# Latent and stick-breaking heads of one layer in one pipeline of head pairs

## The reference, cut to what matters

```python
def block(i):                       # stick-breaking, 128 queries
    z = einsum('bhqd,bhkd->bhqk', qb, k) * scale
    mask = k_idx[None, :] < q_idx[:, None]
    log_beta = log_sigmoid(z)
    log_1m_beta = where(mask, log_sigmoid(-z), 0.0)
    suffix = cumsum(log_1m_beta, reverse=True) - log_1m_beta
    a = where(mask, exp(log_beta + suffix), 0.0)
    return einsum('bhqk,bhkd->bhqd', a, v)

def even_mixer(...):
    mla = causal_softmax_attention(q, k, v, MLA_QK ** -0.5)
    sb = stick_breaking_attention(sq, sk, sv)
    return concatenate([merge_heads(mla), merge_heads(sb)], -1) @ w_o
```

## Time and profile before

| | |
|---|---|
| median of 3 runs | 2231.72 us |
| profiled execution | 2235.53 us |
| its span | 2233.8 us |
| PE, PEld busy | 93%, 75% |
| DVE, ACT, POOL busy | 40%, 25%, 49% |
| granted TensorE clock, mean | 0.941 |
| `att2` | from 997.5 us to 1046.2 us of the span |
| `stk` | from 1046.2 us to 1156.3 us |
| `x2` and `out2` begin | 1156.8 us and 1159.6 us |
| `fox` | from 1736.1 us to 1816.1 us |

### The profile page before, as it was taken

How to read it: one execution, slowest core, us unless ns; L and a number is a source line. 1 busy time by engine, 2 the same in 40 slices (tenths; PEclk the granted TensorE clock), 3 DMA queues, 4 the chain that set the end, 5 groups by cost and what they waited for, 6 DMA issues and landing times.

```text
span 2233.8 us, 30365 instructions
## 1 busy us (share of the span) xinstructions
PE 2066.8 (93%) x10488; PEld 1671.8 (75%) x10488; DVE 883.7 (40%) x1588; ACT 552.6 (25%) x1376; POOL 1084.4 (49%) x703
## 2 busy tenths in 40 slices
PE   5776999789999998979999999999899899999999
PEld 4666676678888887757668888888688568888887
DVE  4664567255434016456664212100462634121200
ACT  2111556232223003336542101000221522011100
POOL 5443003247666655400025766656465345666663
PEclk9886998889999999989569999999999999999999
DMA  4212001123233223210012333323232012333322
GB/s 137 64 61 66 0 0 38 40 64 104 94 97 119 86 81 89 64 38 1 1 38 76 104 94 98 99 85 103 54 100 85 30 39 72 108 94 95 102 91 88
DMA packets 125372, 161.96 MB, mean 73 GB/s; under 512 B 11670, under 2 KB 87398, under 8 KB 125286
## 3 DMA queue, kind: packets, MB, share of 16 engines
q1 hardware_dynamic: 121440, 159.97, 22.8%
q10 hardware_dynamic: 3846, 0.82, 0.2%
HBM read 158.66 MB, written 2.10 MB: 72 GB/s over the span
## 4 chain that ended last, share of the span: by engine, by line
PE 85%; DVE 8%; ACT 3%; issue 2%; POOL 1%; DMA 1%; ACTq 0%; SPq 0%; DVEq 0%; POOLq 0%
PE ps L653 22%; PE ps L654 22%; PE ps L655 22%; PE ps L1061 5%; PE ps L1082 4%; PE ps L1073 2%; PE ps L668 2%; PE ps L786 1%; PE ps L1066 1%; PE ps L1011 1%; DVE tok L1768 1%; PE ps L1089 1%; PE ps L1190 1%; DVE xt_lo L1778 1%; ACT dump L1309 1%
## 5 line engine op out<-in xcount | busy, mean ns | idle before, releaser
L435 POOL TENSOR_TENSOR w_lo<-raw,w_hi 128x1024 fp32r<-128x1024 f32 (+1 forms) x256 | 614.9, 2402 | 21.3
L433 POOL TENSOR_SCALAR w_hi<-raw 128x1024 fp32r<-128x1024 f32 (+1 forms) x256 | 276.0, 1078 | 546.6 <-PE ps L655 530.2
L653 PE MATMUL ps<-xt_hi,w_hi 128*128 128x512 f32 (+1 forms) x1160 | 434.2, 374 | 7.2 <-DVE xt_lo L1778 6.4
L654 PE MATMUL ps<-xt_lo,w_hi 128*128 128x512 f32 (+1 forms) x1160 | 433.4, 374 | 0.0
L655 PE MATMUL ps<-xt_hi,w_lo 128*128 128x512 f32 (+1 forms) x1160 | 433.2, 373 | 0.0
L653 PE MATMUL ps<-w_hi,xt_hi 128*128 128x512 f32 (+3 forms) x672 | 263.5, 392 | 28.8 <-ACT tok L1604 19.4
L654 PE MATMUL ps<-w_lo,xt_hi 128*128 128x512 f32 (+3 forms) x672 | 259.0, 385 | 0.0
L655 PE MATMUL ps<-w_hi,xt_lo 128*128 128x512 f32 (+3 forms) x672 | 258.9, 385 | 0.0
L653 PEld LDWEIGHTS ps<-xt_hi,w_hi 128*128 128x128 f32 x1160 | 220.5, 190 | 47.1 <-DVE xt_lo L1778 7.6
L655 PEld LDWEIGHTS ps<-xt_hi,w_lo 128*128 128x128 f32 x1160 | 220.3, 190 | 38.5
L654 PEld LDWEIGHTS ps<-xt_lo,w_hi 128*128 128x128 f32 x1160 | 220.4, 190 | 38.4
(11 more groups left out here) (310 smaller groups left out, 2771.4 us busy)
## 6 DMA issues: line engine op xcount, KB each, us to landing
raw<-in_w_up SPq DMA_DIRECT2D x88, 256.0 KB
raw<-in_l_w_gate SPq DMA_DIRECT2D x88, 256.0 KB
raw<-in_l_w_up SPq DMA_DIRECT2D x88, 256.0 KB
raw<-in_l_w_down SPq DMA_DIRECT2D x40, 512.0 KB
raw<-in_l_w_in SPq DMA_DIRECT2D x36, 512.0 KB
raw<-in_w_down SPq DMA_DIRECT2D x20, 512.0 KB
raw<-in_l_w_o SPq DMA_DIRECT2D x16, 512.0 KB
raw<-in_w_in SPq DMA_DIRECT2D x12, 512.0 KB
```

Of the source, the lines that this page charges most:

```text
L433: e.tensor_scalar(w_hi[:, s, 0:width], r, 1.0, 0.0, ALU.mult, ALU.add).then_inc(split, 1)
L435: e.tensor_tensor(w_lo[:, s, 0:width], r, w_hi[:, s, 0:width].bitcast(F32), ALU.subtract).then_inc(split, 1)
L653: e.matmul(o, s_hi, m_hi, start=start, stop=False)
L654: e.matmul(o, s_hi, m_lo, start=False, stop=False)
```

## The change

`att2`, `stk` and `x2` are gone. One pipeline `mix` of 8 pairs takes their place, in the form of `fox`: pairs 0 to 3 are the latent heads (`soft`), pairs 4 to 7 the stick-breaking ones. The class `Pairs` gives the rounds of both `fox` and `mix`; 32 steps (a pair's 4 blocks of 512, 384, 256 and 128 keys) run in 40 rounds, the weights of a soft step are turned 2 rounds after its scores, those of a stick step 3 rounds after. `fox` keeps its order on every engine.

- The latent heads' scores contract 96 rows, so the two heads of a pair can't lie above each other; they run one after the other. Their keys lie in `km_a` and `km_b`.
- A stick step: PE scores of two heads side by side (queries and keys 128 rows high, `qs` and `ksb`, now 4 tiles of 128 rows turned with half as many transposes), ACT Sigmoid of the negated scores, DVE a running product from the row's end into `runs` (`products`), POOL the difference of neighbours into the tile of weights (`sticks`), PE transposes, ACT nearly all copies of turned weights (`turner`), PE values. ACT and DVE split the output to high and low (`high`, `low`).
- ACT loads the sigmoid's table before step 16 and the exp and ln table at the end.
- In `act_pair_attend` the copies of turned weights stand ahead of the newest probabilities of the same round.
- POOL splits the four slabs of `out2`'s first group in rounds 3, 7, 11 and 15. SP's order stays, row for row.
- Staging of queries on POOL and the matmuls of no use (`fill` in `stk`) are gone; 8 of them remain at the start.

```diff
-        stage_queries(e, "att2", lambda hd: heads(qm, hd), MQK, 4, ...)
-        stage_queries(e, "stk", lambda hd: heads(qs, hd), HD, 4, [], ("att2", 32))
-        split_all(e, ph["out2"])
+        pool_pairs(e, mix, {3 + 4 * s: (ph["out2"].g0, s) for s in range(4)})
+        split_all(e, ph["out2"], 1)
...
+        def turn_round(self, g):
+            return g + (2 if self.is_soft(g) else 3)
+        def values_round(self, p):
+            return 4 * p + (9 if p < self.soft else 10)
+    fox = Pairs("fox", 8, 8, fox_rooms)
+    mix = Pairs("mix", 4, 8, mix_rooms)
...
+        def sticks(g):
+            for x in range(2):
+                u = 2 * (g - 4 * st.soft) + x + 1
+                e.wait_ge(*at(f"{name}_sc", u))
+                r = run_at(g, x)
+                n = (4 - g % 4) * P
+                e.tensor_tensor(prob_at(g, x), r[:, 1:n + 1], r[:, 0:n], ALU.subtract).then_inc(sem(f"{name}_w"), 1)
...
-        alternate([(64 * i, HD, qs[:, i, :]) for i in range(8)]),
+        alternate([(P * i, P, qs[:, i, :]) for i in range(4)]),
...
+    def turner(st, g, y):
+        if st.is_soft(g):
+            return "a" if y == 1 and g % 4 in (0, 3) else "d"
+        return "d" if y == 0 and g == 4 * st.soft + 3 else "a"
...
+    def mix_scores(e, p, i, b):
+        n = (i + 1) * P
+        if p < mix.soft:
+            for x in range(2):
+                hd = 2 * p + x
+                e.matmul(bank(b[x], n), qm[:, hd, i * P:(i + 1) * P], (km_a, km_b)[hd // 4][:, hd % 4, 0:n],
+                         start=True, stop=False)
+            for x in range(2):
+                m = e.matmul(bank(b[x], P, i * P), ident_b[:, :], causal[:, :], start=False, stop=True)
+            return m
+        for x, r in enumerate(HALVES):
+            e.matmul(bank(b[x], n), qs[r, p - mix.soft, i * P:(i + 1) * P], ksb[r, p - mix.soft, 0:n],
+                     start=True, stop=False)
+        return half_masks(e, b, i * P, strict, strict_x)
...
-        pe_attend(e, att["att2"])
-        pe_attend(e, att["stk"])
-        pe_out(e, "out2", "x2_lo", ...)
+        pe_pair_attend(e, mix, mix_scores, heads_of(v2), [at("in2_tpa", 12), at("in2_tpd", 15), at("in2_copy", 32)], [])
+        pe_out_direct(e, "out2", [at("mix_lo", 2), at("mix_lo", 4), at("mix_slo", 2), at("mix_slo", 4)], ...)
...
+                else:
+                    e.wait_ge(*at(f"{name}_s", g + 1))
+                    e.activation(prob_at(g, x), src, ACT.Sigmoid, scale=-1.0).then_inc(*od.done(*done))
...
+        for r in st.rounds:
+            if r == 4 * st.soft and r < st.steps:
+                e.preload_act_table(ACT.Sigmoid)
+            for g in st.turned_in(r):
+                turned(g)
+            for p in st.pair_in(r, st.inverse_round, range(st.soft)):
+                inverses(p)
+            if r < st.steps:
+                probs(r)
...
+        def products(g):
+            n, h = (4 - g % 4) * P, g - 4 * st.soft
+            for x in range(2):
+                e.wait_ge(*at(f"{name}_p", 2 * g + x + 1))
+                if h >= 4:
+                    e.wait_ge(*at(f"{name}_w", 2 * (h - 4) + x + 1))
+                e.tensor_tensor_scan(run_at(g, x)[:, 0:n][:, ::-1], prob_at(g, x)[:, ::-1],
+                                     one[:, 0:1].broadcast_to([P, n]), 1.0, ALU.mult, ALU.mult).then_inc(
+                    *od.done(*at(f"{name}_sc", 2 * h + x + 1)))
```

More of the change, by code:

```diff
@@ L493, in widened, with halves @@
             e.tensor_copy(inv_w[:, :, :], inv[:, :].unsqueeze(2).broadcast_to([P, 8, HD])).then_inc(sem(f"{name}_iw"), 1)
[L495 to L500, removed]
+        def halves(p):
             e.wait_ge(*at(f"{name}_x", p + 1))
@@ L506, in pool_pairs @@
                 sem(f"{name}_lo"), 1)
+        def sticks(g):
[6 more added lines that the diff above has]
+        for r in st.rounds:
+            for p in range(st.soft):
+                if r == 4 * p + 5:
+                    widened(p)
+            if r in slabs:
+                split_slab(e, *slabs[r], SLAB)
+            for p in range(st.soft):
+                if r == max(4 * p + 11, st.inverse_round(p) + 2):
+                    halves(p)
+            if st.is_soft(r - 1) or r - 1 >= st.steps:
+                continue
+            sticks(r - 1)
     def stage_queries(e, ph, q_src, rows, iters, ready, before=None):
@@ L592, in _ @@
         e.tensor_copy(pick[:, :, :], pick8[:, :].unsqueeze(2).broadcast_to([P, 8, P])).then_inc(picks, 1)
-        pool_pairs(e, "fox", 8, {s: (ph["out3"].g0, s) for s in range(4)})
+        pool_pairs(e, fox, {9 + 4 * s: (ph["out3"].g0, s) for s in range(4)})
         split_all(e, ph["out3"], 1)
@@ L1033, in pe_pair_attend, with half_masks @@
-            if g >= 9 and g % 4 == 1:
-                values((g - 9) // 4)
+                    e.wait_ge(*is_turned(st, st.steps - 1, y))
+                    e.wait_ge(*at(f"{name}_r{'ad'[y]}", st.pairs - 1))
+                turn_inverses(st.pairs - 1).then_inc(sem(f"{name}_ri"), 1)
+            for p in st.pair_in(r, st.values_round, range(st.pairs)):
+                values(p)
+    HALVES = (slice(0, HD), slice(HD, P))
+    def half_masks(e, b, last, mask, mask_x):
+        for x, r in enumerate(HALVES):
+            e.matmul(bank(b[x], P, last), ident_b[r, :], mask[r, :], start=False, stop=False)
+        for x, r in enumerate(HALVES):
+            m = e.matmul(bank(b[x], P, last), ident_x[r, :], mask_x[r, :], start=False, stop=True)
+        return m
@@ L1046, in fox_scores @@
-        for x, r in enumerate(halves):
-            m = e.matmul(bank(b[x], P, last), ident_x[r, :], causal_x[r, :], start=False, stop=True)
-        return m
+        return half_masks(e, b, i * P, causal, causal_x)
     def pe_attend(e, cfg):
@@ new lines, in high @@
+        def high(p):
+            e.wait_ge(*at(f"{name}_o", p + 1))
+            e.activation(xt_hi[:, p, :], bank(6), ACT.Copy).then_inc(*od.done(*at(f"{name}_shi", p + 1 - st.soft)))
+        for r in st.rounds:
+            if r == 4 * st.soft and r < st.steps:
+                e.preload_act_table(ACT.Sigmoid)
+            for g in st.turned_in(r):
+                turned(g)
+            for p in st.pair_in(r, st.inverse_round, range(st.soft)):
+                inverses(p)
+            if r < st.steps:
+                probs(r)
+            for p in range(st.soft, st.pairs):
+                if r == st.values_round(p) + 1:
+                    high(p)
@@ L1576, in _ @@
+        if st.soft < st.pairs:
+            e.preload_act_table_set(EXP_LN)
     @block.scalar
@@ new lines, in low @@
+        def low(p):
+            e.wait_ge(*at(f"{name}_shi", p + 1 - st.soft))
+            e.tensor_tensor(xt_lo[:, p, :], bank(6), xt_hi[:, p, :].bitcast(F32), ALU.subtract).then_inc(
+                *od.done(*at(f"{name}_slo", p + 1 - st.soft)))
+        for r in st.rounds:
+            if r == 4 * st.soft and r < st.steps:
+                e.wait_ge(*at(f"{name}_s", r + 1))
+                for g in range(r, r + 4):
+                    n = (4 - g % 4) * P
+                    e.memset(runs[:, :, RUN_AT[g % 4] + n:RUN_AT[g % 4] + n + 1], 1.0).then_inc(*od.own())
+            if r < st.steps:
+                (maxima if st.is_soft(r) else products)(r)
+            for p in range(st.soft):
+                if r == 4 * p + 4:
+                    inverses(p)
+            for g in st.turned_in(r):
+                turned(g)
+            for p in st.pair_in(r, st.inverse_round, range(st.soft)):
+                turned_inverse(p)
+            for p in range(st.soft):
+                if r == max(4 * p + 10, st.inverse_round(p) + 1):
+                    scaled(p)
+            for p in range(st.soft, st.pairs):
+                if r == st.values_round(p) + 1:
+                    low(p)
```

316 lines of the change are left out of this document (128 added, 188 removed).

## The result

| | before | after |
|---|---|---|
| median (lowest to highest) | 2231.8 us (2231.17 to 2232.52, 4 runs) | 2167.09 us (2165.19 to 2172.37, 4 runs) |
| profiled execution, its span | 2235.53, 2233.8 us | 2167.14, 2165.3 us |
| first scores of the new pipeline's place | 997.53 us | 994.01 us |
| first matmul of `out2` | 1159.57 us | 1095.50 us |
| last low part before `up2` | 1224.46 us | 1158.77 us |

The ratio is 0.9714, 95% interval 0.9697 to 0.9731: 64 us faster. The forecast was 2162, range 2148 to 2180. The stage that was 162.0 us long is 101.5 us long (forecast 97.5).

A forecast was written before the change was run, and what follows sets the result against it. Stick half before: a loop through four engines at PE's low clock; after: DVE and POOL excluding each other. Stage 162.0 to 97.5 us (-64.5), with -1.9 and -3.5 together -69.9: 2165.6 profiled, 2162 median, range 2148 to 2180.

The forecast's parts named there:

- the way out: End of the stage: a short transposition, two copies and one pair's values, 4.5 us in all.
- the way in: From step 16's scores to the first running product: about 2 us, the table's load standing beside the scores.
- the soft half: Latent heads, pairs 0 to 3: 10.2 us a pair, bounds 9.3 and 11.5; step 16's scores 36.0 us after the start.
- the stick half: Stick-breaking pairs 4 to 7: 13.0 us a pair, bounds 11.3 and 16; 52 us for four, plus 3 for POOL's leftovers.
- `in2`, -3.5 us: Input projection: half as many transposes of stick-breaking queries and keys, 3.5 us less, bounds 0 and 3.6.
- The exclusion: Stick half: DVE's products and POOL's differences block each other; 13.6 us a pair, or 11.3 with 0.14 us overlap per handover.
- The difference in DVE's queue: Stick half: if DVE made the subtraction instead of POOL, both would be in one queue at the same sum.
- `x2` and `out2`, -1.9 us: Output projection: without `x2`'s transposes, first matmul to last low part falls from 64.9 to 63.0 us, 1.9 less.
- From the profiled execution to the median: Whole run: the median lies 3.8 us below the profiled execution, so 2165.6 us becomes 2162.
- no exclusion: Rival, stick half: DVE and POOL don't block each other; 9.3 us a pair, 15 us less, 2147; chance 0.1.
- PE at the low clock: Rival, stick half: PE stays at 1.2 GHz and is the bound; 16 us a pair, 12 more, 2174; chance 0.2.
- third rival: Stick half: ACT's copies of step r - 3 before step r's sigmoids collapse the look-ahead; 33 us a pair, 2242; chance 0.02.

The follow-up runs named there:

- the same without PSUM: Fastest kernel of the study, but its running products read the sigmoids from SBUF again instead of PSUM: 2156.55 us, stage 89.0, against 2148.48 us, stage 81.5.
- the fastest kernel: Changed kernel plus sigmoids before ACT's copies, products from PSUM, pair 6's values early in bank 7, DVE's copies before products: 2148.48 us against 2167.09.
- tail run: Changed kernel with the values of pair 6 in round 31 instead of 34 and in bank 7: 2164.38 us against 2167.09, stage 98.0 against 101.5.

## Why the prediction was right, and where not

The time was right, 2162 against 2167.1. The stage came out at 101.5 us for 97.5, but that it is only 4 us off is in part luck: the way out took 5.6 us more than its term and the way in and the soft half 1.9 more, against 3.6 less in the stick half. By its steps:

- `in2`, -3.5 us. The rows bear it out by durations: 64 transposes of 64 columns took 7.3 us, their 32 successors 3.8; and the run with the 32 issued twice was slower. The mark of the first scores moved from 997.53 to 994.01 too, but that shows nothing: in the kernels of this study that are the same up to there it stands between 990.7 and 998.4.
- The soft half: 10.37 us a pair for 10.2. Step 16's scores (1030.70) come 36.7 us after the start for 36.0. Right.
- The way in, 2 us. It was 3.2 (1033.92 - 1030.70). The table's load did not stand beside the scores: it began only after step 15's exponentials, at 1031.99, and the sigmoid 1.30 later. The drain behind the load that the Trainium skill names (ScalarE: Activation LUTs, What ACT_TABLE_LOAD costs) does not show: the sigmoid begins 0.02 us after the load's end.
- The stick half, 52 us for four pairs and 3 for leftovers. It was 51.4 in all. The sum was right, its split was not. The exclusion is real, and what it alone sets is some 10.8 us a pair (the third pair of the same without PSUM), where the working gave 11.3. That these are so near is luck too: I had taken POOL's difference too long (1.27 for 1.04 us), so 13.6 should have been 12.2 and 11.3 about 10.0, and a handover gains less than the 0.14 us that I took, about 0.09 us. I took 13.0 for a pair because of PE's clock. But holding the clock up in most stretches took 1.1 us off the half, ACT's order alone 4.2, and ACT's order and DVE's copies together 7.2 us (51.4 to 44.2). The low clock was for the most part a consequence of these waits: in the fastest kernel, without fillers, it does not come. I had priced that loop as a rival at 33 us a pair or nothing; it came in part, some 4 us over the half.
- The difference in DVE's queue, "at the same sum". That was wrong: there it takes 0.67 us for 512 columns, so DVE's whole work on a pair would be some 10.5 us by the rows of that run, and the stick half came out 2.3 us shorter.
- The way out, 4.5 us. This step failed: it was 10.1 us, from the last product's end (1085.36) to 1095.50. The working had the values of pair 7 only. Those of pair 6 also come after the last turn, in round 34, at the low clock (4.49 us), and hold the one output bank for 1.5 us more. The tail run took 3.5 us of that back.
- `x2` and `out2`, -1.9 us. From the first matmul to the last low part it is 63.3 us (1158.77 - 1095.50) against 64.9 before and the 63.0 forecast, and 63.0 to 63.4 in ten of the thirteen profiles of the changed kernel and its variants; it was 61.8 in one and 59.4 in two (last section). Right.
- From the profiled execution to the median I took off 3.8 us. The two profiled spans differ by 68.5 us, the medians by 64.7. Up to the last low part the profiles give 3.5 + 60.6 + 1.6 = 65.7; the other 2.8 us lie in stages that did not change, in an execution of the kernel before that was 3.7 us above its median. So taking them off was right.

Of the rivals, no exclusion is out: taking it away brought 6.2 us, and 8.1 where the loop was gone. PE at the low clock is out as the bound: holding it up in most stretches brought 0.9 us, within the spread. The third rival's sign was there, ACT waiting for turned weights in nearly every round, and that should have stood in the sum.

## What to carry to other kernels

Where DVE and POOL work side by side, give DVE's operation at most one operand in SBUF; writing ACT's result back into its PSUM bank was enough here, and worth 7.5 to 9 us of a stage of 89 to 101. In a pipeline written out by hand, let each engine issue first what feeds the engine that is waited for: the newest sigmoids on ACT, but the oldest copies on DVE where PE stood waiting for them. And for the end of a pipeline write down what each engine still has in its queue, and which single buffers it shares; a period times a count leaves that out.

## What the runs showed of the hardware

The exclusion also makes one kernel's runs differ. Here are two executions of the changed kernel, the same code, in the norm behind `out2`. First DVE, then POOL, in the timeline of the one:

```profile
1144.76 0.96 DVE L1801 SCALAR_TENSOR_TENSOR rstd<-sq_a,rstd 128x2 f32<-128x2 f32 x1
1145.76 4.68 DVE L1825 SCALAR_TENSOR_TENSOR tok<-h,rstd,gains 128x1024 f32<-128x1024 f32 x2
```

```profile
1144.67 1.06 POOL L445 TENSOR_SCALAR w_hi<-raw 128x1024 fp32r<-128x1024 f32 x1 [1.02 <-DMA raw<-in_l_w_up]
1145.81 2.36 POOL L447 TENSOR_TENSOR w_lo<-raw,w_hi 128x1024 fp32r<-128x1024 f32 x1
```

and of the other:

```profile
1144.40 0.16 DVE L1801 SCALAR_TENSOR_TENSOR rstd<-sq_a,rstd 128x2 f32<-128x2 f32 x1
1144.60 5.28 DVE L1825 SCALAR_TENSOR_TENSOR tok<-h,rstd,gains 128x1024 f32<-128x1024 f32 x2
```

```profile
1144.41 1.07 POOL L445 TENSOR_SCALAR w_hi<-raw 128x1024 fp32r<-128x1024 f32 x1 [1.13 <-DMA raw<-in_l_w_up]
1145.57 3.23 POOL L447 TENSOR_TENSOR w_lo<-raw,w_hi 128x1024 fp32r<-128x1024 f32 x1
```

An operation on two columns takes 0.96 us instead of 0.16, and ends as POOL's does (1145.72 and 1145.73); POOL had come 0.09 us before it. In the other execution DVE came 0.01 us first. The first of its two operations on L1825 then took 1.96 us in the chain instead of 3.50, POOL's second 3.23 us instead of 2.36, and the stretch of `out2` up to its last low part is 59.4 us long instead of 63.3. PE's transposes behind it come 2.3 us earlier, counted from `out2`'s first matmul; and in the slower execution PE had waited 2.49 us for them and its granted clock then was 0.50 from 1150 to 1152 us, which makes the other 1.5 us. The thirteen profiles agree: in the two of 59.4 us no operation on two columns is stretched there, in each of the other eleven one takes 0.90 to 1.03 us, and in the one of 61.8 among these the clock stayed at 1.0. A tenth of a microsecond in who issues first sets which. Steps of 2 to 4 us between executions of one kernel can come from that; that all do was not tried.

The exclusion holds for the running product too, whose second operand in SBUF is one column of ones, broadcast. The earlier trace rows had shown it for the running sum of 384 columns; the sums of 512 and 256 columns on either side of it in that trace, also beside POOL's splits of slabs, took 2.36 and 2.68 us instead of 1.22 and 0.69.
